# A two-layer block whose experts stream from HBM: four homes instead of three for each pair's weights

## What is computed

```python
def grouped_moe(h, router_w, router_b, w_gate, w_up, w_down):
    ...
    for e in range(N_EXPERTS):
        hid = jax.nn.silu(h @ w_gate[e]) * (h @ w_up[e])
        out = out + gate[..., e:e + 1] * (hid @ w_down[e])
    return out
```

## Time and profile before

| | |
|---|---|
| median of three runs | 1636.36 us (1635.1 to 1639.24) |
| the profiled execution: time | 1637.5 us |
| its span, first to last instruction | 1635.7 us |
| PE (matmul) busy | 1546.1 us, 95% |
| PE weight load busy | 1113.5 us, 68% |
| VectorE busy | 809.3 us, 49% |
| ScalarE busy | 543.9 us, 33% |
| moved by DMA | 346.64 MB, mean 212 GB/s |
| TensorE's granted clock, mean | 0.985 |

### The profile page before, as it was taken

How to read it: one execution, slowest core, us unless ns; L and a number is a source line. 1 busy time by engine, 2 the same in 40 slices (tenths; PEclk the granted TensorE clock), 3 DMA queues, 4 the chain that set the end, 5 groups by cost and what they waited for, 6 DMA issues and landing times. The chain is left out here.

```text
span 1635.7 us, 23769 instructions
## 1 busy us (share of the span) xinstructions
PE 1546.1 (95%) x9625; PEld 1113.5 (68%) x9625; DVE 809.3 (49%) x1712; ACT 543.9 (33%) x1007; POOL 0.5 (0%) x7
## 2 busy tenths in 40 slices
PE   7998999999999999999989989989999989899999
PEld 5856745444476774544437666888999964599897
DVE  6897721111244672111126267686666537565544
ACT  3445211111124521111113355334343322644443
POOL 0000000000000000000000000000000000000000
PEclk9999999999999999999999988999999999999999
DMA  9531689999952368999992000205443754013552
GB/s 323 199 129 31 225 341 430 428 429 427 364 192 91 105 232 332 430 429 428 428 364 80 1 1 1 106 1 213 148 180 133 263 195 154 1 52 121 188 205 77
DMA packets 83728, 346.64 MB, mean 212 GB/s; under 512 B 8240, under 2 KB 15280, under 8 KB 71360
## 3 DMA queue, kind: packets, MB, share of 16 engines
q1 hardware_dynamic: 76272, 338.28, 53.0%
q10 hardware_dynamic: 7376, 7.26, 1.4%
HBM read 344.48 MB, written 1.05 MB: 211 GB/s over the span
## 5 line engine op out<-in xcount | busy, mean ns | idle before, releaser
L826 PE MATMUL ps<-ring,arena 128*64 128x512 f32 (+6 forms) x1728 | 380.4, 576 | 18.2 <-DMA ring<-in_w_up 11.6
L826 PEld LDWEIGHTS ps<-ring,arena 128*64 128x64 f32 (+2 forms) x1728 | 135.2, 142 | 244.0 <-issue 238.1
L826 PE MATMUL ps<-arena_r,ring_r 128*128 128x272 f32 (+1 forms) x896 | 256.3, 286 | 0.0
L1838 ACT ACTIVATE arena<-ps 128x512 f32<-128x512 f32 (+7 forms) x161 | 73.4, 480 | 375.0 <-PE ps L826 177.1
L826 PEld LDWEIGHTS ps<-arena_r,ring_r 128*128 128x128 f32 x896 | 169.3, 189 | 0.0
L826 PE MATMUL ps<-arena_r,y_r 128*128 128x272 f32 (+1 forms) x560 | 157.1, 286 | 4.3 <-issue 1.6
L826 PE MATMUL ps<-arena_r,ff_hi_r 128*128 128x272 f32 (+1 forms) x576 | 119.9, 291 | 1.7 <-DVE hT L2479 1.4
L2485 DVE SCALAR_TENSOR_TENSOR arena<-arena,small,ps 128x512 f32<-128x512 f32 x16 | 12.0, 748 | 216.6 <-PE ps L826 216.6
L826 PE MATMUL ps<-h_r,y_r 128*128 128x256 f32 (+1 forms) x400 | 113.5, 284 | 0.0
L826 PEld LDWEIGHTS ps<-arena_r,y_r 128*128 128x128 f32 x560 | 104.6, 189 | 5.8 <-issue 2.0
L2479 DVE TENSOR_TENSOR ring_r<-ring,y_r 128x1024 fp32r<-128x1024 f32 x74 | 89.0, 1222 | 35.9 <-ACT y_r L1838 35.9
(11 more groups left out here) (337 smaller groups left out, 2348.1 us busy)
## 6 DMA issues: line engine op xcount, KB each, us to landing
ring<-in_w_gate SPq DMA_DIRECT2D x32, 2048.0 KB, 15.8
ring<-in_w_up SPq DMA_DIRECT2D x32, 2048.0 KB, 17.2
ring<-in_w_down SPq DMA_DIRECT2D x32, 2048.0 KB, 13.3
ring<-in_w_ff SPq DMA_DIRECT2D x32, 2048.0 KB, 9.1
ring<-in_w_in SPq DMA_DIRECT2D x8, 2048.0 KB, 19.2
ring<-in_w_in_ab SPq DMA_DIRECT2D x5, 2048.0 KB, 12.7
ring<-in_w_o SPq DMA_DIRECT2D x4, 2048.0 KB, 10.4
ring<-in_ple_gate SPq DMA_DIRECT2D x4, 2048.0 KB, 8.5
```

What stands on the lines that cost most here:

```text
L826: return pe.matmul(o, lhsT, rhs, start=a, stop=z)
L1838: return act.activation(o, i, ACT.Copy, scale=scale)
```

## The change

The pair homes become four (`HOMES`), one of them outside the ring, and the matrices of the stream take them in turn whatever they are: matrix pair n of a layer (gate, up, down of turn 0, gate of turn 1, ...) lives in home n mod 4. Homes 0, 1 and 2 are the slots (0, 3), (1, 4) and (2, 5). Home 3 is `SPARE`: for expert d = 0 `hT_t` and two stretches of `arena`, for d = 1 `y_t` and `edge_t`, four pieces of 1024 float32 a partition each.

- A load into home 3 is made by `spare_load`, with three DMAs for d = 0 and two for d = 1, on a semaphore of its own, `spare_full`.
- The gate pair of turn 1 (n = 3) is loaded into home 3 ahead of the stage: its half for d = 1 right behind the down load of d = 0, the other behind the down load of d = 1.
- `pair_load` loads pair n when pair n - 4 has been used, for n = 4 to 23. Before, it was when pair n - 3 had been used.
- The turn number decides where a matrix is, so TensorE's and SyncE's turns are written out (seven ahead of the branch; four to a loop body in the crowded rounds). VectorE and ScalarE keep their loops.
- `wait_last_experts` and SyncE's waits in the false side follow the new homes.
- To have a semaphore for `spare_full`, `ppT_ev` and `rt_ev` are made into one, `p_and_scores`.

```diff
+        SPARE = [
+            [hT_t[:, 0:DM], hT_t[:, DM:2 * DM], view(8192, DM), view(12416, DM)],
+            [y_t[:, 0:DM], y_t[:, DM:2 * DM], edge_t[:, 0:DM], edge_t[:, DM:2 * DM]],
+        ]
+        HOMES = NSLOT // 2 + 1
+
+        def expert_weights(home, d, at):
+            if home < HOMES - 1:
+                at += (3 * d + home) * SLOT_W
+                return ring[:, at:at + 512]
+            return SPARE[d][at // DM][:, at % DM:at % DM + 512]
...
+            def turns(R, r, n):
+                if not by_home:
+                    with eng.Fori(0, n) as i:
+                        turn(R, r, i, True)
+                elif n < PAIRS:
+                    for i in range(n):
+                        turn(R, r, i, True, i, 0)
...
-            with eng.Fori(0, PAIRS - 1) as i:
-                turn(R, 0, i, True)
+            turns(R, 0, PAIRS - 1)
...
             def wait_last_experts(l, n):
                 last = l * ROUNDS * NE + NE
-                if n % 3 < 2:
-                    sp.wait_ge(gu_mm, last - 1 + n % 3)
+                if n % 3 == 0:
+                    sp.wait_ge(dn_mm, last - 2)
                 else:
-                    sp.wait_ge(dn_mm, last)
+                    sp.wait_ge(gu_mm, last - 2 + n % 3)
...
+                def spare_load(src, d):
+                    if d == 0:
+                        sp.dma_start(hT_t[:, 0:2 * DM], src[:, 0:2 * DM]).then_inc(spare_full, 16)
+                        sp.dma_start(SPARE[d][2], src[:, 2 * DM:3 * DM]).then_inc(spare_full, 16)
+                        sp.dma_start(SPARE[d][3], src[:, 3 * DM:4 * DM]).then_inc(spare_full, 16)
+                    else:
+                        sp.dma_start(y_t[:, :], src[:, 0:2 * DM]).then_inc(spare_full, 16)
+                        sp.dma_start(edge_t[:, 0:2 * DM], src[:, 2 * DM:4 * DM]).then_inc(spare_full, 16)
...
-                expert_loads(l * ROUNDS, 0, 1)
+                    if j == 2:
+                        spare_load(A["w_gate"][l, 3 - d], 1 - d)
+
+                def pair_load(R, g, n):
+
+                    i, j = n // 3, n % 3
+                    home, i0, j0 = n % HOMES, (n - HOMES) // 3, (n - HOMES) % 3
+                    at = g * (2 * HOMES) + R * NE
+                    if j0 < 2:
+                        sp.wait_ge(gu_mm, at + (2 * i0 + 1 + j0))
+                    else:
+                        sp.wait_ge(dn_mm, at + (2 * i0 + 2))
...
+                for n in range(HOMES, 3 * MOE_TURNS):
+                    pair_load(l * ROUNDS, 0, n)
...
+                    sp.wait_ge(spare_full, SPARE_LOAD * HOME_LOADS * (l * ROUNDS + 1))
...
+                                w = expert_weights((3 * a + j) % HOMES, d, at + k * step)
+                                ins = mm(ps[e, bank, :], x[:, k, e], w, k == 0, k == chunks - 1)
```

More of the change, by code:

```diff
@@ L44 @@
 PAIRS = NE // 2
+HOME_LOADS = 3 * PAIRS // 4
 JOBS = NE + 2
@@ L506, in program @@
         slot_full = [sem(f"slot_full{i}") for i in range(NSLOT)]
+        spare_full = sem("spare_full")
         setup_done = sem("setup_done")
@@ L547, in program @@
         MOE_TURNS = NE // 2
+        SPARE_LOAD = 16 * 5
         EXPERT_PARTS = (("w_gate", KC), ("w_up", KC), ("w_down", FC))
@@ L646, in program, with rounds @@
         W_COLS = [(0, MLA_IN), (COL_DQ, DIFF_W), (COL_DK, DIFF_W), (COL_DV, 512), (COL_SQ, 2 * SB_W), (COL_SV, SB_W)]
-        def rounds(eng, l, begin, turn, end, spare, close=None):
+        def rounds(eng, l, begin, turn, end, spare, close=None, by_home=False):
+            def turns(R, r, n):
[6 more added lines that the diff above has]
+                else:
+                    with eng.Fori(0, n // HOMES) as g:
+                        for a in range(HOMES):
+                            turn(R, r, g * HOMES + a, True, a, g)
+            last = (PAIRS - 1, 0) if by_home else ()
             eng.wait_ge(crowd_ready, l + 1)
@@ L653, in rounds @@
             begin(R, 0)
-            with eng.Fori(0, PAIRS - 1) as i:
-                turn(R, 0, i, True)
+            turns(R, 0, PAIRS - 1)
             with eng.If(crowded == 1):
-                turn(R, 0, PAIRS - 1, True)
+                turn(R, 0, PAIRS - 1, True, *last)
                 end(R, True)
@@ L660, in rounds @@
                     begin(r + R, r)
-                    with eng.Fori(0, PAIRS) as i:
-                        turn(r + R, r, i, True)
+                    turns(r + R, r, PAIRS)
                     end(r + R, True)
@@ L666, in rounds @@
             with eng.Else():
-                turn(R, 0, PAIRS - 1, False)
+                turn(R, 0, PAIRS - 1, False, *last)
                 end(R, False)
@@ L722, in _ @@
                         gate_of_embedding(1)
[L724 to L734, removed]
-                expert_loads(l * ROUNDS, 0, 1)
+                    if j == 2:
[6 more added lines that the diff above has]
+                        sp.wait_ge(gu_mm, at + (2 * i0 + 1 + j0))
+                    else:
+                        sp.wait_ge(dn_mm, at + (2 * i0 + 2))
+                    for d in range(2):
+                        src = A[EXPERT_PARTS[j][0]][l, bass.ds(g * (2 * HOMES) + (2 * i + d), 1)].rearrange("e p w -> (e p) w")
+                        if home < HOMES - 1:
+                            sp.dma_start(whole_slot(3 * d + home), src).then_inc(slot_full[3 * d + home], 16)
+                        else:
+                            spare_load(src, d)
+                for n in range(HOMES, 3 * MOE_TURNS):
+                    pair_load(l * ROUNDS, 0, n)
                 sp.wait_ge(crowd_ready, l + 1)
@@ L741, in _ @@
                     with sp.Fori(1, ROUNDS) as r:
-                        expert_loads(r + l * ROUNDS, r, 0)
+                        with sp.Fori(0, MOE_TURNS // HOMES) as g:
+                            for n in range(3 * HOMES):
+                                pair_load(r + l * ROUNDS, g, n)
                     sp.wait_ge(dn_mm, NE * ROUNDS * (l + 1))
@@ L1190, in begin, with turn, both @@
                             mm(ps[:, g, :], zeros[:, 0:P], zeros[:, 0:512], True, False)
-                def turn(R, r, i, more):
-                    def both(bank, x, n, j, chunks):
+                def turn(R, r, i, more, a, g):
+                    def both(bank, x, j, chunks, at, step):
                         for k in range(chunks):
@@ L1238, in turn @@
                             pe.wait_ge((xg1_ev, xg0_ev)[half], i + R * (PAIRS + 1) + 2)
-                        both(4 + half, hidT, lambda n: slot(n, FC)[:, :, half * 512:half * 512 + 512], 2, FC).then_inc(dn_mm, 1)
+                        both(4 + half, hidT, 2, FC, half * 512, DM).then_inc(dn_mm, 1)
                 def end(R, more):
@@ L3474, in slot_count @@
 def slot_count(n, l):
-    per = 16 * (NE // 2) * ROUNDS + 16 + (16 if n != 3 else 0)
+    per = 16 * HOME_LOADS * ROUNDS + 16 + (16 if n != 3 else 0)
     return l * per
```

41 lines of the change are left out of this document (23 added, 18 removed).

## The result

The changed kernel takes 1618.27 us, median of six runs (1616.8 to 1622.31), against 1634.74 us for six runs of the kernel before (1630.42 to 1639.24). The ratio is 0.9904, 95% interval 0.9882 to 0.9925: 16 us, or 1.0%, less. Measured again, it took 1619.37 us, with a ratio of 0.9902 (0.9887 to 0.9917).

The account below looks back on a forecast made before the run. Full DMA engines in both expert stages were taken as the bound, a turn's loads taking 29.3 us against PE's 27.43. Removing the up waits (-11.5 us) gave 1626.0 from the profile, 1624.9 from the median; forecast 1625.4 us, range 1621 to 1632.

Parts of the forecast that it names:

- All eight waits: PE's stops ahead of the up products in turns 3 to 6, both layers; all were to go.
- The start of the sum: Profiled execution 1637.5 us and median 1636.36; less 11.5 they gave 1626.0 and 1624.9, and 1625.4 between them was taken.
- the brackets: Idle times in PE's timeline ahead of up products: 0.57, 1.71, 1.72, 1.71 us; 5.7 and 5.8 us a layer.
- the slow stretch behind the jump: Gate and up of turn 7 at granted clock 0.50 behind the jump, costing 1.70 us; expected to stay.
- The first term of the sum, -11.5 us: Fourth home removes all four up waits in each expert stage: -(5.7 + 5.8) = -11.5 us.
- The jump stays, and with it, as a rule, the slow stretch behind: Ahead of turn 7 on PE: stops of 2.24 and 2.1 us remain, usually with the slow clock behind.
- Rival 4: Slow stretches or the jump's stop vanish too: 1622 for the clock alone, 1618 with the stops; chance 6%.
- DMA's price for home 3: Five DMAs with shorter pieces instead of two in each home-3 load: +0.3 us a load and no wait.
- The spare time in the prediction: Lead of up loads over PE in turns 5, 6 and 7 of layer 0: 5.8, 4.2 and 4.9 us.
- A fixed part of about 1 us per DMA: Rival 1, home-3 loads: 3 us more each, at worst even at 1636; 6% within 0.3%, 2% slower.
- never over 428: DMA rate in GB/s, given as the reason that below the price bound for home-3 loads lies no gain.
- Code loads that stop PE: Rival 2, written-out turns: late code pieces stop PE 2.2 or 3.9 us each; 6% slower, 3% within 0.3%.

Follow-up runs that it names:

- the turns written out: Kernel before with TensorE's seven turns written out and three homes kept: 1643.01 us, ratio 1.0045.
- small pieces: Changed kernel with each home-3 load in 16 DMAs of 512 columns instead of 5 DMAs: 1622.43 us, ratio 0.9922.
- `w_in` held back: Changed kernel with every load for the next stage waiting for the last down product: 1619.93 us, ratio 0.99.

## Why the prediction was right and wrong

**The bound and the mechanism: right.** DMA is full, PE runs away from it by 1.9 us a turn, and a lead of one pair carries it to the end. All eight waits went, in the turns named, and the run with the fourth home filled late gives all of it back.

**What failed: the sizes of three terms of the sum.** The result lies 7.1 us below the forecast. The start of the sum was 2.2 us too high, the waits for up were worth more than the brackets say (1.8 us more in the first trace of the kernel before, 0.8 in the second), and the slow stretch behind the jump, which was put at no change, came less often (1.7 us in the first pair of traces, 3.4 in the second). That is 5.7 us of the 7.1 by the first pair and 6.4 by the second.

**The first term of the sum, -11.5 us: mis-sized.** It was read from the brackets of the timeline, which count from the modelled end of the matmul before. The start of one up to the start of the next says more: 385.38 - 356.02 = 29.36 us against 27.43 for a turn without wait, so a wait of "1.71" costs 1.93. The prediction had this 1.9 us a turn in its second paragraph and then summed the brackets. By starts it is 0.79 + 3 x 1.93 = 6.6 us in layer 0 and 6.7 in layer 1, 13.3 in all.

**"The jump stays, and with it, as a rule, the slow stretch behind": half right.** The jump stayed (2.26 us by starts). The slow stretch didn't in layer 0, and that is 1.70 us. 13.3 + 1.7 is 15.0 of the 15.2 us by which the two stages became shorter. In the second pair of traces both slow stretches are gone: the stages are 231.4 us twice against 223.7 and 223.5, 15.6 us shorter, and 12.3 + 3.4 is 15.7.

Why it comes less often is open. Where the waits of turns 4 to 6 were there, a slow stretch stood behind the jump in seven of eight places (two traces of the kernel before, one with the late fourth home, one with the turns written out, where layer 0 has the second stop). Where they were gone or nearly so, it was three of eight (two traces of the changed kernel, small pieces, `w_in` held back). But the length of the stop sorts the places as well: behind the stops of 1.98 to 2.24 us it stood in nine of eleven, behind the four of 1.74 to 1.90 us in none, and three of these four are in kernels without the waits. No run tells the two apart. In runs without a trace it can't be seen: the mean granted clock is 0.987 in the runs of both kernels, and the slow stretches between 950 and 1110 us, which are far from the change, vary by more.

Rival 4 had 1622 without the slow stretches and 1618 with the stops gone too, at 6%. The measured time is its 1618, but that is chance: the stops stayed, and the rest came from the brackets and from the start of the sum.

**The start of the sum.** The median of the three runs shown was 1636.36; over six it is 1634.74, and the midpoint with the profiled execution put another 0.5 on it: 2.2 us in all.

**DMA's price for home 3: right in the stream, too small at its end.** 423 GB/s instead of 426, and a turn 0.2 us longer in the late-fourth run; taken was 0.3 a load. Up of turn 6 has four such loads ahead of it or in it, so by this price it lands at 375.5 + 1.2 = 376.7, and it did at 376.6. The spare time in the prediction doesn't have this price in it. Up of turn 7 would be at 406.0 and landed at 406.9. PE also came 1.7 us earlier than the prediction said, so 1.1 us were left to spare and not 4.9, and without the jump up of turn 7 is waited for. The last 0.9 us stand beside the jump: that pair lands 9.8 us behind the gate pair in both four-home kernels whose TensorE doesn't jump ahead of turn 7, and 10.8, 11.1 and 10.1 us in three traces with the jump. How the jump delays it wasn't tried.

**The rivals.** A fixed part of about 1 us per DMA: fallen. Three more DMAs and shorter packets cost 0.3 us a load, eleven more 0.85, and in the small pieces' own stretch the rate is that of 2 KB packets in large DMAs. The prediction put beside this rival the Trainium skill's rule of 1 MiB or more (DMA: Bandwidth & Descriptors, section Bandwidth), which gave +2.5 us a load; measured is 0.3, so the figure for DMAs issued from GpSimd does not carry over to this queue, which is never empty. Two readings beside it were off, without weight in the sum: three quarters of a home-3 pair come in DMAs of 1 MB, not half, and the page before has slices with 430 GB/s, where the prediction says never over 428.

Code loads that stop PE: fallen for straight code (1634.5 against 1633.5), but the jump was underrated: the kernels with it lost 7.4 us in one case and some 14 in another. That the changed kernel pays only 2 us a layer for it is luck, and the forecast had no term for it. The rule of the Trainium skill on taken branches (Runtime: NRT & Kernel Launch, section Instruction fetch mechanics) agrees with the traces in that it is the branch and not the straight code that stops PE.

**What stays open.** The medians differ by 14.8 to 16.5 us. The waits (12.3 to 13.3) and the slow stretches (1.7 to 3.4) give 15.0 to 15.7 in the two pairs of traces, so no other cause is needed. Open are why slow stretches come less often in the changed kernel, and what made the jump so dear in two of the kernels.

## What to carry to other kernels

Where loads and compute have nearly the same pace and the stage is short, buffers are worth what can be put into them before the stage begins, not their number. Here four homes gained nothing without that (1635.6 us) and some 15 us with it: look for stretches in which DMA stands still ahead of the stage and for dead SBUF to fill then. Price a wait by the step between starts of the same work with and without it, not by the idle time in front of it. And when the code grows or is reordered, look at each far jump afterwards: two kernels with the same products and loads were 7 and 14 us slower here, and not so without the jump or with it elsewhere.

## What the runs showed of the hardware that was not expected

- The stop behind a far jump on TensorE took 1.7 to 2.2 us in most kernels, 1.8 + 4.6 us in one, and 7.4 to 8.5 us at the end of a layer, with the next loads filling the queue in small packets. PE went on 2.6 to 3.6 us after the last piece of code began on q8, in nearly all places 2.8 to 2.9.
- TensorE's clock went to 0.50 behind nine of eleven jump stops of 1.98 to 2.24 us (2.04 us without, 2.02 with), and behind three of four waits for up of over 2 us (2.05, 2.21 and 2.71 us with, 2.36 without). It never did behind the waits of 1.7 us in these traces.
- In a full queue issued by SyncE, DMAs of 256 KB and DMAs of 1 to 2 MB, both in 2 KB packets, ran at the same 387 GB/s; loads of 2 MB in long packets ran at 426.
